# Modulation of the first two channel tiles made tile by tile at the start of a two-block transformer kernel

## What is computed

```python
mx = [m[:, None, :] for m in jnp.split(jax.nn.silu(c) @ w_mod[l] + b_mod[l], 6, axis=-1)]
mc = jnp.split(jax.nn.silu(c_ctx) @ w_mod[l] + b_mod[l], 6, axis=-1)
hx = modulate(rmsnorm(x, g_norm1[l]), mx[0], mx[1])      # h * (1 + scale) + shift
hc = modulate(rmsnorm(ctx, g_norm1[l]), mc[0], mc[1])
px = jnp.split(hx @ w_in[l], IN_SPLIT_IDX, axis=-1)
pc = jnp.split(hc @ w_in[l], IN_SPLIT_IDX, axis=-1)
```

## Time and profile before

| | us |
|---|---|
| median of three runs | 822.99 (822.92 to 823.28) |
| the profiled execution, first to last instruction | 821.9 |
| TensorE busy in it | 797.3 |
| VectorE, ScalarE, GpSimd busy | 428.3, 418.8, 376.9 |

### The profile page before, as it was taken

The page is one execution under the profiler, slowest core; times in us unless marked ns, Lnnn a source line. Parts: engine busy times, 40 slices in busy tenths (PEclk is TensorE's granted clock), DMA queues, the critical chain, the costliest instruction groups (busy, mean ns, idle before and its releaser), DMA issues.

```text
span 821.9 us, 14292 instructions
## 1 busy us (share of the span) xinstructions
PE 797.3 (97%) x5493; PEld 695.4 (85%) x5493; DVE 428.3 (52%) x684; ACT 418.8 (51%) x641; POOL 376.9 (46%) x181
## 2 busy tenths in 40 slices
PE   6999999999899999999999999999999999999996
PEld 4778877887778999999998889999887988899985
DVE  4675568984667533422336747645455333423435
ACT  5335426455846444444444955654756544444443
POOL 3126000000164654666545986565464554666452
PEclk9999999999999999999999999999999999999999
DMA  9984577134953666555654796434455556566551
GB/s 320 302 285 133 161 235 253 54 102 103 345 168 116 198 193 190 175 179 185 192 166 132 227 205 186 130 105 132 150 167 167 157 182 197 180 190 191 184 149 51
DMA packets 94397, 146.61 MB, mean 178 GB/s; under 512 B 15742, under 2 KB 64111, under 8 KB 94353
## 3 DMA queue, kind: packets, MB, share of 16 engines
q1 hardware_dynamic: 92896, 143.23, 55.9%
q0 software_dynamic: 1424, 2.77, 1.3%
q10 hardware_dynamic: 32, 0.01, 0.0%
HBM read 144.93 MB, written 1.06 MB: 178 GB/s over the span
## 4 chain that ended last, share of the span: by engine, by line
PE 85%; DVE 6%; issue 3%; POOL 2%; ACT 2%; DMA 2%; DVEq 0%; SPq 0%; ACTq 0%; POOLq 0%
PE bank L1877 82%; POOL w_lo L628 2%; ACT w_hi L693 1%; PE bank L2147 1%; PE bank L1968 1%; DMA raw<-in_w_mod 1%; DMA x<-in_x 1%; DMA gate_mlp_b<-gate_rows 1%; DVE x L1829 1%; PE bank L2455 1%; DVE w_lo L1196 1%; DVE stat L1513 1%; DVE x L1642 0%; DVE o_lo L1734 0%; DVE bank L1641 0%
## 5 line engine op out<-in xcount | busy, mean ns | idle before, releaser
L628 POOL TENSOR_TENSOR w_lo<-raw,w_hi 128x1024 fp32r<-128x1024 f32 (+2 forms) x150 | 361.8, 2428 | 318.7 <-ACT w_hi L693 318.5
L693 ACT ACTIVATE w_hi<-raw 128x1024 fp32r<-128x1024 f32 (+1 forms) x218 | 226.1, 1045 | 217.3 <-PE bank L1877 192.5
L1196 DVE TENSOR_TENSOR w_lo<-raw,w_hi 128x1024 fp32r<-128x1024 f32 x71 | 87.0, 1236 | 141.3 <-ACT w_hi L693 141.2
L1877 PE MATMUL bank<-z_hi,w_hi 128*128 128x256 f32 x384 | 109.0, 284 | 0.2
L1877 PE MATMUL bank<-z_hi,w_lo 128*128 128x256 f32 x384 | 107.2, 279 | 0.0
L1877 PE MATMUL bank<-z_lo,w_hi 128*128 128x256 f32 x384 | 107.1, 279 | 0.0
L1877 PE MATMUL bank<-n_hi,w_hi 128*128 128x256 f32 x352 | 100.4, 285 | 1.0 <-POOL w_lo L628 1.0
L1877 PE MATMUL bank<-n_hi,w_lo 128*128 128x256 f32 x352 | 99.8, 284 | 0.0
L1877 PE MATMUL bank<-n_lo,w_hi 128*128 128x256 f32 x352 | 99.0, 281 | 0.0
L1877 PE MATMUL bank<-w_hi,mlp_h_hi 128*128 128x512 f32 x216 | 85.3, 395 | 0.0
L1877 PE MATMUL bank<-w_hi,mlp_h_lo 128*128 128x512 f32 x216 | 85.2, 395 | 0.0
(11 more groups left out here) (419 smaller groups left out, 1553.0 us busy)
## 6 DMA issues: line engine op xcount, KB each, us to landing
raw<-in_w_in SPq DMA_DIRECT2D x54, 512.0 KB, 4.5
raw<-in_w_down SPq DMA_DIRECT2D x54, 512.0 KB, 3.7
raw<-in_w_gu SPq DMA_DIRECT2D x44, 512.0 KB, 3.5
raw<-in_w_up SPq DMA_DIRECT2D x32, 512.0 KB, 3.7
raw<-in_w_mod SPq DMA_DIRECT2D x24, 512.0 KB, 4.1
raw<-in_w_mod SPq DMA_DIRECT2D x32, 256.0 KB, 6.1
raw<-in_w_out SPq DMA_DIRECT2D x12, 512.0 KB, 4.0
raw<-in_w_in SPq DMA_DIRECT2D x8, 336.0 KB, 3.0
```

Of the source, the lines that this page charges most:

```text
L628: nc.gpsimd.tensor_tensor(wl[:, w % SPL, 0:size], raw[:, slot_raw, 0:size], wh[:, w % SPL, 0:size].bitcast(F32), ALU.subtract).then_inc(s_ ...
L693: nc.scalar.activation(wh[:, w % SPL, 0:size], raw[:, slot_raw, 0:size], ACT.Copy).then_inc(s_hi, 1)
L1196: V.tensor_tensor(wl[:, w % SPL, :], raw[:, slot_raw, :], wh[:, w % SPL, :].bitcast(F32), ALU.subtract).then_inc(s_lod, 1)
L1877: return nc.tensor.matmul(out_, l, r_, start=start, stop=stop, skip_group_check=True)
```

## The change

- `w_mod`'s columns for tile 0 and for tile 1 are loaded apart, in two chunks each of four loads with pieces of 512 bytes (`add_mod_one`). The list of chunks now begins: 0 and 1, `w_mod` for tile 0; 2, FF of tiles 0 and 1; 3, HQ of tiles 0 and 1; 4 and 5, `w_mod` for tile 1; 6 to 9, `w_mod` for tiles 2 and 3; from 10 on it is as before. The modulation has five steps m in place of four groups (`MODS`).
- For tiles 0 and 1 ACT copies the row (`row_copy`, 256 columns) in place of DVE. The DVE arithmetic on the columns is now of pieces of two columns from PSUM, the scale first.
- x's 1/rms is made before the context's squares, both from the one function table that has Ln and Exp, so that one table load is gone; the diagonals and the spreading matmul are made for x and the context apart. Tile 0's product reads the spread factors from PSUM.
- `h_f` and `h_hi` of a tile are waited for by halves (x, context) in place of both.
- The FF chunk's low part for tiles 0 and 1 is made in two halves (`ff_low`). Its slot counts as released when the second half is made ("ff lo rest").
- On PE the first pass of the loop is written out: products by kind (hi x hi of tile 0, then hi x lo, then lo x hi), with the modulation's matmuls between, and HQ of tile 0 before FF of tile 1. `mod_cols(2)`, the columns for tiles 2 and 3, stands last, behind all products of tiles 0 and 1. The loop over j begins at 1.

```diff
-        add_mod(0)
+        add_mod_one(0)
         for j in range(4):
             add_in(2 * j, 2, FF_AT, 512)
-            if j < 3:
+            if 0 < j < 3:
                 add_mod(j + 1)
             add_in(2 * j, 2, HQ_AT, 512)
+            if j == 0:
+                add_mod_one(1)
+                add_mod(1)
...
+        MODS = ((0, 1, 0), (1, 1, 2), (2, 2, 4), (4, 2, 8), (6, 2, 12))
...
             if kind == "w":
                 low_made(eng, i)
+                if i == 0:
+                    eng.wait_ge(DV.sem, DV["ff lo rest"])
...
-            load_functions(LN)
+            load_functions(LN_EXP)
...
+                if t % 2:
+                    act.wait_ge(AC.sem, AC[f"sq {t}"])
+                    ln_exp(act, 67 + t, 63 + t, 2, D, f"1 {t // 2}")
...
+            modulation(0)
+            h_product(0, 0)
+            ff_low(0, lambda ins: ins.then_inc(s_lod, 1))
+            h_low(0)
+            x_from_psum(1, 2)
+            chunk_lo(1, number["w"][1] % RAW)
+            modulation(1)
             dve.wait_ge(AC.sem, AC["x rstd"])
-            h_product(0)
-            chunk_lo(0, number["w"][0] % RAW)
-            h_low(0)
-            h_product(1)
+            h_product(1, 1)
+            ff_low(1, lambda ins: tick(ins, "ff lo rest"))
             h_low(1)
...
+            pe.wait_ge(s_hi, 1)
+            pe.wait_ge(AC.sem, AC["hh 0 1"])
+            forget(0, 0)
+            mod_rows(1, (0,))
+            split(0)
+            forget(0, 1)
+            pe.wait_ge(DV.sem, DV["hl 0"])
+            forget(0, 2, (0, 1))
+            mod_rows(1, (1,))
+            forget(0, 2, (2, 3))
+            split(1)
+            pe.wait_ge(AC.sem, AC["x rstd"])
+            pe.wait_ge(DV.sem, DV["xT 1 2"])
+            query(1, 0, (0, 1))
+            mod_cols(1)
+            query(1, 0, (2, 3))
+            pe.wait_ge(AC.sem, AC["hh 1 1"])
+            forget(1, 0)
+            mod_rows(2, (0,))
+            pe.wait_ge(DV.sem, DV["ff lo rest"])
+            forget(1, 1)
+            pe.wait_ge(DV.sem, DV["hl 1"])
+            forget(1, 2).then_inc(s_used, 1)
+            mod_rows(2, (1,))
+            query(1, 1).then_inc(s_used, 1)
+            mod_cols(2)
+            w_at[0] = 2
+            for j in range(1, 4):
```

More of the change, by code:

```diff
@@ L319, in add_mod, with add_mod_one @@
                 add("mod", *[(mod_pairs[:, k + j, :, 256 * g:256 * g + 256], 0, P, 2, 256) for j in range(2)])
+        def add_mod_one(k):
+            for half in range(2):
+                add("mod", *[(mod_pairs[:, 4 * half + j, :, P * k:P * k + P], 0, P, 2, P) for j in range(4)])
         def add_acc(b, k):
@@ L732, in _ @@
                     hi(1)
+                elif k == 1:
+                    act.wait_ge(PE.sem, PE["x rstd 1"])
+                    nc.scalar.activation(rowb[:], ps[5][:], ACT.Copy).then_inc(AC.sem, AC.tick("x rstd"))
+                    hi(2)
+                    row_copy(1)
                 elif k == 2:
@@ L1215, in x_from_psum @@
                                    ps[XT_BANKS[v][pair]][:].rearrange("p (k t) -> p k t", k=2)), f"xT {v} {pair}")
[L1217 to L1224, removed]
-                    ins = V.tensor_scalar(dg4[:, t, :], ident, stat[:, 68 + t:69 + t], None, ALU.mult)
[L1226 to L1231, removed]
+            for pair in range(4):
+                x_from_psum(0, pair)
@@ new lines, in x_diagonals, with modulation @@
+            def x_diagonals(v):
+                dve.wait_ge(AC.sem, AC[f"rstd 1 {v}"])
+                for t in (2 * v, 2 * v + 1):
+                    ins = V.tensor_scalar(dg4[:, t, :], ident, stat[:, 68 + t:69 + t], None, ALU.mult)
+                tick(ins, f"x diag {v}")
+            def modulation(m, lows=()):
+                k0, n, _ = MODS[m]
+                if m >= 2:
+                    dve.wait_ge(s_mod, MODS[m][2] + 4)
+                    tick(V.tensor_copy(modrow[:, m % 2, :], ps[6][:]), f"row {m}")
@@ L1239, in modulation @@
[L1239 to L1243, removed]
+                dve.wait_ge(PE.sem, PE[f"mod t {m}"])
+                at_ = 160 + 4 * k0
+                for k in range(k0, k0 + n):
+                    c = at_ + 2 * (n + k - k0)
+                    ins = V.tensor_scalar(modc[:, 8 + k, :], ps[7][:, c:c + 2], stat[:, 240 + k:241 + k], cols[:, R_G1 + k:R_G1 + k + 1],
+                                          ALU.add, ALU.mult)
@@ L1924, in _, with row_made @@
             nc.tensor.transpose(ps[7][:, 0:16], rowsc[0:16, :], ident[0:16, 0:16]).then_inc(PE.sem, PE.tick("c rows"))
[L1926 to L1936, removed]
+            def row_made(m):
+                if m < 2:
+                    pe.wait_ge(AC.sem, AC[f"row {m}"])
+                else:
+                    pe.wait_ge(DV.sem, DV[f"row {m}"])
@@ new lines, in mod_cols, with mod_rows @@
+            def mod_cols(m):
+                k0, n, _ = MODS[m]
+                row_made(m)
+                for q in range(2 * n):
+                    at_ = 160 + 4 * k0 + 2 * q
+                    ins = mm(ps[7][:, at_:at_ + 2], modrow[:, m % 2, P * q:P * q + P], cst[:, C_SEL:C_SEL + 2], True)
+                ins.then_inc(PE.sem, PE.tick(f"mod t {m}"))
+            def mod_rows(m, halves=(0, 1)):
+                k0, n, c0 = MODS[m]
+                if m:
+                    row_made(m - 1)
@@ L2019, in _, with forget, query @@
             to_hq = [(ps[4 + j // 2][:, T * (j % 2):T * (j % 2) + T], j % 2 == 0) for j in range(4)]
-            keep_clock(0, 2)
-            for j in range(4):
+            def forget(k, product, tiles=range(HG)):
+                assert k < 2
+                l, r_ = ((wh, hh), (wl, hh), (wh, hl))[product]
+                for h in tiles:
+                    c = 512 * (k % 2) + P * h
+                    ins = mm(ps[h][:], l[:, 0, c:c + P], r_[:, k, :],
+                             k == 0 and product == 0, k == KT - 1 and product == 2)
+                return ins
+            def query(w, k, tiles=range(4)):
+                s = w % SPL
+                for j in tiles:
+                    o, first = to_hq[j]
+                    c = 512 * (k % 2) + P * j
+                    ins = mm3(o, wh[:, s, c:c + P], wl[:, s, c:c + P], hh[:, k, 0:T], hl[:, k, 0:T], first and k == 0, k == KT - 1)
+                return ins
+            pe.wait_ge(s_hi, 1)
[26 more added lines that the diff above has]
+            for j in range(1, 4):
                 s = split(w_at[0])
```

95 lines of the change are left out of this document (56 added, 39 removed).

## The result

The changed kernel takes 831.87 us, median of 4 runs (830.52, 830.63, 833.11, 835.02), beside 822.95 of the kernel before (822.59 to 823.28, 4 runs): ratio 1.0106, interval 1.0084 to 1.0128. It is slower, by 8.9 us, where 6.0 were forecast; the time lies 0.3 above the top of the predicted range, so the range did not hold it.

What follows compares the result with a forecast made beforehand. PE was taken to bound the kernel, busy 797.3 of 821.9 us. Terms -1.6 + 1.2 + 2.5 + 3.5 + 0.4 = +6.0 gave 827.9, plus 1.1 outside the span 829.0 us; range 825.3 to 831.6.

Steps and rivals of the forecast that it cites:

- The start: Kernel start up to PE's first product: at 17.8 us, 4.2 earlier than 22.04.
- The half speed of loads that I feared for 512-byte pieces: Rival: w_mod chunks of tiles 0 and 1 load at half of 358 GB/s, PE waits 2.9; 831.9 us, chance 0.05.
- The work between the first product and tile 2's start: PE products and modulation there take 13.25 us; without waits tile 2 starts at 31.05, a gain of 1.6.
- Waits 1 to 3: PE waits before tile 2's start: 1.2 for tile 1's h, 2.5 for chunk 9, 3.5 for tile 2's h.
- wait 2: PE waits 2.5 us (1.2 to 3.2) for chunk 9, as SP can't issue chunk 8 before "ff lo rest".
- wait 3: PE waits 3.5 us for tile 2's h, with nothing between the columns and tile 2.
- The 6.3 taken for chunk 9: Within the wait for chunk 9: it lands 6.3 us after the first load is issued into the empty queue.
- Wait 4: PE's existing wait for tile 4's h grows by 0.4 us (0 to +1), as chunks 15 and 16 land later.
- The clock: Rival: PE's clock falls to 1.2 GHz in the new waits, +1.9 us (0 to +3.5); 830.9 us, chance 0.12.
- Outside the span: Timed runs lie 1.1 us above the profiled execution's span; this was added to 827.9.
- The direction: Whole kernel: slower, chance 0.91, beside same 0.05 and faster 0.04.

Runs made afterwards that it cites:

- a_low_whole: Changed kernel with the low part of FF's first chunk made whole at once, and SP's wait on "ff lo rest" gone; 828.48 us.
- b_cols_late: Kernel before with only the columns for tiles 2 and 3 moved behind HQ of tile 1, directly ahead of tile 2; 828.79 us.
- the filled kernels: Kernels given unused matmuls in PE's waits: the changed kernel 830.36 us, a_low_whole so filled 825.98 us, b_cols_late so filled 827.03 us.
- b_cols_late_filled: b_cols_late with six unused matmuls behind the moved columns; 827.03 us.
- a_filled: Changed kernel with unused matmuls on PE: four ahead of tile 2's second half-row, six behind its columns; 830.36 us.
- a_rows_early: a_low_whole with tile 2's rows and columns taken ahead of tile 1's last products; 824.77 us.
- a_kinds: a_rows_early with tile 2's and 3's products ordered by kind, the next rows between them, FF's second low part behind tile 2's products; 824.34 us.
- a_again: The changed kernel run and profiled once more, with no edit; 832.26 us.

## Why the prediction was wrong

**The start** was right: first product at 17.65 (forecast 17.8), 4.4 earlier than before. The half speed of loads that I feared for 512-byte pieces is not there: 1 MB of them landed between 9.30 and 12.88 us, 293 GB/s, not half of 358. That rival falls; that its 831.9 is the time measured is chance.

**The work between the first product and tile 2's start** was 0.9 too small: 21.31 us lie between them, less the waits 7.14, is 14.2 in place of 13.25. It is spread over the stretch (0.4 up to the first wait, 0.4 to the second, 0.1 to the third); the same sum made for the kernel before gives 10.4 for the 10.6 in its trace, so durations put in a row come out short, and I passed over that. The sentence that most of the 4.2 earned is modulation work moved into the products holds, and more so: with no wait at all the change would gain 0.8 us, not 1.6.

**Waits 1 to 3** were right in place, releaser and size: 1.08, 2.70 and 3.36 beside 1.2, 2.5 and 3.5. That their causes are those named is shown: a_low_whole takes SP's hold away and wait 2 goes, while wait 3 stays at 3.27; b_cols_late puts the columns there in the old kernel and makes a wait of 3.32. Tile 2's start came at 38.96, forecast 38.2; the 0.9 of work, less 0.15 at the start, is the difference. Two figures beside the terms were wrong: scaling the 7.0 us of the earlier trace rows from 300 to 358 GB/s gives 5.9, not 5.0, and the bounds of the single terms add to 826.5 to 831.1, not to 827.0 to 830.6. The 6.3 taken for chunk 9 was near the 6.7 measured, though not because an empty queue is slow (a_low_whole).

**Wait 4** was wrong in sign. I took tile 4's h to be set by the late chunks 15 and 16 and gave +0.4. Tile 4 doesn't wait at all in after, where it waited 0.57 before, so the term is -0.6 and the step failed by 1.0. The half clock in tile 2 is not the reason, since the wait is gone in the filled kernels too. In the kernel before, the small column operation of 1.80 ends at 41.88, and POOL's low parts, running since 37.13, end at 41.86. With tile 2 late, the columns come behind POOL's low parts. In b_cols_late_filled, which has the old arithmetic, the same operation takes 0.17. The rows are POOL's of the kernel before, then POOL's and DVE's of b_cols_late_filled:

```profile
37.13 4.73 POOL L628 TENSOR_TENSOR w_lo<-raw,w_hi 128x1024 fp32r<-128x1024 f32 x2 [29.44 <-ACT w_hi L693]
```

```profile
37.99 4.73 POOL L628 TENSOR_TENSOR w_lo<-raw,w_hi 128x1024 fp32r<-128x1024 f32 x2 [30.26 <-ACT w_hi L693]
44.71 0.17 DVE L1239 SCALAR_TENSOR_TENSOR mod_cols<-mod_cols,cols 128x4 f32<-128x4 f32 x1
```

In after POOL is done at 48.35 and the columns begin at 48.77. Where the new columns, read from PSUM, do meet POOL (a_filled, a_rows_early, a_kinds), they take their 0.5 and 0.3 us and the first product behind them, with two inputs in SBUF, is held instead (1.58, 1.93 and 2.58 us where others last 0.48), as the prediction argued. That DVE is held by POOL is read from these end times; no run moves POOL's low parts alone.

**The clock** is the step that failed, and the reason why the range did not hold the time. I held the granted clock at 1.00 for the likeliest case, so that the sum had nothing for it, and gave its fall 0.12, at +1.9. Behind PE's third wait it fell in all four profiles in which that wait was 3.2 to 3.4 us (after, a_again, a_low_whole, b_cols_late), each time for 6.8 us at 1.2 GHz. Its price up to tile 4's start is the difference in growth between three pairs of kernels: 1.75 and -0.5 (a_again, a_filled), 1.66 and -0.67, 1.76 and -0.68, so 2.3 to 2.4 us; the medians of the pairs, which hold what reaches the end, differ by 1.9, 2.5 and 1.8. The level dropped inside the wait, 1.6 to 2.2 us after PE had stopped, and not at its end. The rival was sized nearly right and given too little. The Trainium skill ("TensorE: Matmul & The Clock Gate", "Why this matters for your kernels"), which says that idle gaps between bursts bring the half clock back, is borne out by the third wait of these traces, though not by the 3.16 us of a_again's second; the trace of before, whose longest wait was 1.6, could not decide it, and I let it count as evidence against, which it was not.

**Outside the span** I took 1.1 us, from the profiled span to the median. In every timed execution since, of every kernel, time and span differ by 1.8. So the profiled execution of the kernel before was about 0.7 us slower than its median (an estimate: 821.9 + 1.8 beside 822.95), and the 1.1 was 1.8 less that. As only this offset was added to an old span plus a difference, the forecast lost nothing by it against the median of before.

**The account.** From 6.0 to 8.9: +0.7 at tile 2's start, -1.0 at wait 4, +2.4 for the clock, together +2.1, or +8.1 in all, beside the +8.15 that the two traces show at tile 4. That the miss is no larger is in part luck: wait 4 took back 1.0 of what the clock and the work added. The 0.8 that are left lie between the profiled pair and the medians. Later falls of the clock, as in a_again near 228 us, are a likely part of them, but no run isolates them, and this stays open.

**Slower or faster.** The direction was right for the reason given. The new order asks PE for modulation before it has products enough to cover what hangs on it.

## What to carry to other kernels

When work moves so that the bound engine gets new waits among its matmuls, give the clock a term of its own in the sum: here it fell in four of four waits of 3.3 to 3.4 us, in neither of the waits of 2.70 and 3.16, and a fall cost 2.3 us up to tile 4. Products placed between an operation that makes scale factors and the tile that uses them are worth as much as the chain behind it is long (3.3 us of waiting here), so look at what stands there before moving either. A wait placed on the engine that issues loads holds all loads behind it; the price is how much later the needed load is issued, less the time for which it would have lain ready: chunk 9 was issued 5.2 us later, and would have been ready 3.3 us before its use (a_low_whole: 26.38 and 29.73).

## What the chip did that was not expected

- After a wait of 3.2 to 3.4 us the clock stayed at 1.2 GHz while PE was busy, for about 5.6 us behind the wait's end, though PE had work without a break (window 40 to 44 of after: PE busy 4.00, PEclk 0.50). What ends a fall the study doesn't show. Nor does it show why the clock held through a_again's wait of 3.16.
- Falls also follow some waits of 1.0 to 1.6 us, in some executions and not in others (b_cols_late_filled at 20 us, a_again near 228 us, a_kinds near 220 us). The wait of 1.64 near 220 to 230 us is in all ten traces, the kernel before's among them, and a fall stands behind it in two, for 3.4 us each time; times of 822.15 to 826.16 for it, with mean clocks of 0.992 to 0.999, go with that.
- A queue that has run empty did not make the loads slower: chunk 9 took 5.8 us from its issue to its landing in after, and 5.4 in a_low_whole, where the queue was full. Between 25.26 and 31.99 us the queue moved 1.6 MB, of which chunks 8 and 9 are 1.
- DVE operations ended with POOL's: 1.79 us for one of 0.17 (before, 41.88 beside POOL's 41.86), and 2.58 for one of 0.48 (a_kinds, 44.07 beside 43.79).
